# Two layers of an attention head loop: VectorE's lower parts ahead of the row maxima, and a landing copy between exponentials

## The chip, the cores and the metric

One NeuronCore of one Trainium2 chip runs the whole model in one launch. The metric is device time in microseconds (us), the median of the runs. The engines are TensorE (PE in the rows, PEld its weight loads), VectorE (DVE), ScalarE (ACT), GpSimd (POOL) and SyncE (SP), which issues the DMAs here. Each engine takes its own instructions in order and waits on semaphores for the others.

## The reference, cut to what matters

272 tokens (256 and 16 meta tokens) go through a convolution layer with a mixture of experts, an MLA attention layer with a mixture of experts, and then through two layers of a second block. The change touches MLA's first projections and, in both layers of the second block, the loop over eight sparse-attention heads:

```python
def mla_mixer(hn, w_dq, cq_g, w_uq, w_o, k_nope, k_rope, v, cos, sin):
    cq = rmsnorm(hn @ w_dq, cq_g)
    ...
for layer in range(DEPTH):                      # second block, twice
    h = rmsnorm_2(x, pre_norm[layer])
    proj = h @ w_in[layer]
    (hq, hf, hi, hz, nq, kc, vc, ks, vs, kw, vw, ng, nz) = jnp.split(proj, offsets, axis=-1)
    o_h = hgrn2_mixer(...)
    o_h = rmsnorm_2(o_h, hgrn_out_norm[layer]).reshape(B, S, HGRN_WIDTH) * jax.nn.silu(hz)
    o_n = nsa_mixer(...)                         # per head: selected and window branch
    ...                                          #   p = softmax(q k' * scale), o += gate * p v
    o_n = o_n.reshape(B, S, NSA_WIDTH) * jax.nn.silu(nz)
    y = jnp.concatenate([o_h, o_n], axis=-1) @ w_out[layer]
    x = x + rmsnorm_2(y, post_norm[layer])
```

## The kernel before

**Weights in two parts.** A weight matrix is cut into units of 128x2048 fp32. SyncE loads a unit in two halves into one of three raw slots of `ring`. ScalarE's `upper` copies each half to fp32r (the upper part, `ring_parts<-ring 128x1024`, line 1187, semaphore `w_hi`); VectorE's `lower_units` subtracts it from the raw half (the lower part, `ring_parts<-ring,ring_parts`, line 1622, semaphore `w_ready`). TensorE then makes every product of three matmuls, `mm3` (lines 532 to 534). The next load into a slot waits until TensorE has used the unit.

**MLA's start.** TensorE multiplies units 16 and 17 (counted over the kernel) by the normed chunks, sums two squares (`norm_sum`, L528), and goes on with unit 18, the third. ScalarE's `mla` takes the root (L1184), makes the upper parts of the 16 chunks as VectorE norms them (`upper_chunk`), then the upper part of unit 18 (`upper(u + 2)`), then copies and squares the first product. VectorE makes the lower part of unit 18 after its last chunk.

**The head loop** (`layer2`, once a layer). Before it, the last two of the unit tiles outside the loop are made, TensorE sums squares for the HGRN norm with four matmuls into banks 4 to 7 (`osum`), ScalarE takes the logarithm of the four banks at once (L1495, `olog`) and then the exponential of it (L1497, `oroot`). Then, for head h = 0 to 7:

- TensorE: `beside(h, 0)`, the first half (a tile) of the projection unit `IN_HEADS[h]`, into bank 7 (h below 6; in heads 6 and 7 there is output projection instead); eight transposes of the probabilities of head h (lines 1108 to 1111, after `p_ready`, signal `pt_done`); `scores(h + 2)`; `beside(h, 1)`, the second tile, again bank 7; the product with v (twelve L528 matmuls, `pv_done`). A tile into bank 7 waits until ScalarE has copied the tile before it out of the bank (`land`, signal `pj_copied`), and for the unit's lower part.
- VectorE: `tensor_copy` of half the transposes (L2151, L2152), `probs(h + 1)` (it scales the exponentials, L2136 to L2139 and an L1642 of 128x512, signal `p_ready`), `maxima(h + 2)` (four reductions L2090 and a scaling L1645, signal `mx_ready`), `lower_next(1)` (the two lower-part instructions of the unit of head h + 1), `output(h)` (L1642 128x256, after `pv_done` and the gate `z_ready`; signal `o_n`). In heads 1, 2, 4 and 5 a gating product of the HGRN output comes first (L1642 128x512, signal `o_h`).
- ScalarE: `land` of tile 0; its half of the transposes; in heads 1, 2, 4 and 5 an upper part of 128x512; `upper` of the unit two heads on; `exps(h + 2)`: four exponentials L1481, two for each branch `br`, after `mx_ready`; `land` of tile 1 (in head 0 it stands ahead of `exps`); in heads 0, 1, 3, 4 and 5 `gate`, Silu on landed tiles (L1472, signal `z_ready`); the upper part of head h's output, after `o_n`. A switch between Exp and Silu costs an ACT_TABLE_LOAD.
- GpSimd: the lower parts of the gated outputs (L1555), each after ScalarE's upper part.

Of the kernel before, what the change touches and what calls it, by code (L numbers as in the profile page):

```python
# [20 lines left out]
P = 128  # L21
D = 1024
# [172 lines left out]
def build(nc, h_in, consts_in, vecs_in, dense, experts, out):  # L195
    with ExitStack() as ctx:
# [190 lines left out]
        def wide(v):  # L387

            return v.rearrange("p a b -> p (a b)")
# [133 lines left out]
        def _(pe):  # L523
# [370 lines left out]
            def layer2(layer):  # L894
# [166 lines left out]
                for i in range(4):  # L1061
                    m = mm(psum[:, 4 + i, :], C("ones"), b_d[:, i * 512:i * 512 + 512], 0, 1)
                m.then_inc(b2["osum"], 1)
# [37 lines left out]
                for h in range(HEADS):  # L1101
                    g, n = h // 4, HEADS * layer + h
                    e, pt = n_e[h % 2], n_pt[h % 2]
                    beside(h, 0)
                    pe.wait_ge(b2["p_ready"], n + 1)
# [63 lines left out]
        def _(act):  # L1169
# [114 lines left out]
            def mla():  # L1284
                norm_root(D, T, 5, loaded=True)
                for parts, whole in ((ml_kvs, ml_kv), (ml_qs, ml_q)):
                    for c in range(DC):
                        t.next(nrm_out)
                        upper_chunk(parts, whole, c)
                u = CONV_UNITS  # L1290
                upper(u + 2)
# [110 lines left out]
            def layer2(layer):  # L1402
# [71 lines left out]
                def exps(h):  # L1474

                    _, least, total = n_st[h % 2]
                    t.next(b2["mx_ready"])
                    for br in range(2):
                        for i, at, n in ((0, 0, P), (1, P, SEQ)):
                            c = 2 * br + i  # L1480
                            m = act.activation(n_e[h % 2][:, br, at:at + n], psum[:, 2 * (h % 2) + br, at:at + n], ACT.Exp,  # L1481
                                               scale=NSA_SCALE, bias=least[:, c:c + 1], accum_out=total[:, c:c + 1])
                    m.then_inc(b2["e_done"], 1)
# [10 lines left out]
                t.next(b2["osum"])  # L1494
                act.activation(wide(b_qe), flat[:, 2048:4096], ACT.Ln, scale=1.0 / P, bias=eps[:, :]).then_inc(b2["olog"], 1)  # L1495
                t.next(b2["olog"])
                act.activation(wide(b_qe), wide(b_qe), ACT.Exp, scale=-0.5).then_inc(b2["oroot"], 1)  # L1497
                exps(1)
                for h in range(HEADS):
# [14 lines left out]
                    if h + 2 < HEADS:  # L1514
                        exps(h + 2)
                    if 0 < h < len(IN_HEADS):
                        land(*IN_HEADS[h], layer, halves=(1,), only=7)
# [88 lines left out]
        def _(v):  # L1606
# [326 lines left out]
            def layer2(layer):  # L1933
# [209 lines left out]
                for h in range(HEADS):  # L2143
# [12 lines left out]
                    if h + 1 < HEADS:  # L2156
                        probs(h + 1)
                    if h + 2 < HEADS:
                        maxima(h + 2)
                    lower_next(1)  # L2160
# [151 lines left out]
```

## Time and profile before

| | us |
|---|---|
| median of 3 runs | 1830.06 |
| lowest, highest | 1828.79, 1831.27 |
| the profiled execution, its own time | 1831.33 |
| its span | 1829.5 |
| TensorE / VectorE / ScalarE / GpSimd busy in it | 1665.1 / 831.9 / 647.7 / 60.2 |
| TensorE's mean granted clock, share of full | 0.948 |

How to read it: the profile is of one execution; times are from the start of its span. MLA's start lies at 587 to 655 us, the head loop of the second block's first layer at 1380.5 to 1463 us and that of the second layer 318.1 us later. Busy time of a pipelined TensorE runs into the next instruction: matmuls start closer than they last. The idle time in brackets is what the engine waited before the row, and the name behind it what ended the wait.

### The profile page before, as it was taken

Reading aid. Unit: us, or ns where it says so; the run is one execution under the profiler, and the core shown is the slowest. Engines: PE = TensorE matmul, PEld = TensorE weight load, DVE = VectorE, ACT = ScalarE, POOL = GpSimd, SP = SyncE. Lnnn points to the kernel's source line nnn. Section 1 sums busy time; section 2 is a strip of 40 time slices with the busy share of each in tenths; the row PEclk is TensorE's granted clock in tenths of the full one; section 3 lists DMA queues with packets and bytes.
Section 4 is the critical chain, followed back from the end, with each engine's and each line's share of the span. In section 5 each row is a group of like instructions: output and inputs, shape, how many; then the busy total and the mean of one; then the engine's idle time right before and its main releaser. Section 6 shows DMA issues by size and latency. Waiting matters only on the chain.

```text
span 1829.5 us, 30992 instructions
## 1 busy us (share of the span) xinstructions
PE 1665.1 (91%) x12314; PEld 1198.2 (65%) x12314; DVE 831.9 (45%) x1503; ACT 647.7 (35%) x1169; POOL 60.2 (3%) x58
## 2 busy tenths in 40 slices
PE   8999888887879999988888888999999999999997
PEld 8995334342425869534343333499998989999897
DVE  5652121221214764322121212388866656886663
ACT  4432111111112643211110111266557645655763
POOL 0100000000001000000000000100001110000110
PEclk9999888888989999989888989999999999999999
DMA  7769999999999524999999999935542344554232
GB/s 283 266 258 415 421 421 421 421 421 422 421 422 418 177 89 168 416 421 421 421 421 421 421 421 422 405 124 175 170 156 93 104 151 130 170 171 153 93 116 93
DMA packets 89660, 527.53 MB, mean 288 GB/s; under 512 B 10080, under 2 KB 10592, under 8 KB 40032
## 3 DMA queue, kind: packets, MB, share of 16 engines
q1 hardware_dynamic: 89568, 526.24, 73.3%
q8 instruction: 66, 1.08, 0.2%
q14 instruction: 26, 0.21, 0.0%
HBM read 525.15 MB, written 1.05 MB: 288 GB/s over the span
## 4 chain that ended last, share of the span: by engine, by line
PE 56%; DMA 26%; DVE 8%; SPq 7%; ACT 2%; issue 1%; DVEq 0%
DMA ring<-experts 25%; PE banks L528 12%; PE banks L532 10%; PE banks L534 10%; PE banks L533 10%; SPq L458 5%; PE banks L728 5%; PE banks L709 3%; PE banks L747 3%; DVE arena L1642 2%; DMA ring<-dense 1%; DVE hT L1767 1%; SPq L465 1%; DVE ring_parts L1622 1%; PE banks L589 1%
## 5 line engine op out<-in xcount | busy, mean ns | idle before, releaser
L532 PE MATMUL banks<-arena_parts,ring_parts 128*128 128x256 f32 (+1 forms) x1444 | 417.1, 289 | 8.2 <-ACT arena L1187 3.9
L534 PE MATMUL banks<-arena_parts,ring_parts 128*128 128x256 f32 (+1 forms) x1444 | 408.7, 283 | 0.0
L533 PE MATMUL banks<-arena_parts,ring_parts 128*128 128x256 f32 (+1 forms) x1444 | 408.2, 283 | 0.0
L728 PE MATMUL banks<-ring,arena 128*32 128x512 f32 x1536 | 252.7, 756 | 119.6 <-DMA ring<-experts 119.5
L528 PE MATMUL banks<-arena 128*128 128x128 f32 (+3 forms) x2416 | 322.9, 288 | 1.9 <-ACT arena L1187 1.3
L528 PEld LDWEIGHTS banks<-arena 128*128 128x128 f32 (+1 forms) x2416 | 289.9, 190 | 47.8 <-issue 35.5
L1187 ACT ACTIVATE arena<-banks 128x256 f32<-128x256 f32 (+9 forms) x366 | 156.5, 454 | 387.7 <-PE banks L740 153.4
L1622 DVE TENSOR_TENSOR ring_parts<-ring,ring_parts 128x1024 fp32r<-128x1024 f32 x204 | 245.2, 1234 | 99.4 <-ACT ring_parts L1187 87.0
L532 PEld LDWEIGHTS banks<-arena_parts,ring_parts 128*128 128x128 f32 x1444 | 272.3, 189 | 16.5 <-issue 7.3
L1187 ACT ACTIVATE ring_parts<-ring 128x1024 fp32r<-128x1024 f32 x208 | 215.3, 1055 | 181.0 <-DMA ring<-dense 179.3
L533 PEld LDWEIGHTS banks<-arena_parts,ring_parts 128*128 128x128 f32 x1444 | 272.6, 189 | 0.3
L534 PEld LDWEIGHTS banks<-arena_parts,ring_parts 128*128 128x128 f32 x1444 | 272.2, 188 | 0.0
L728 PEld LDWEIGHTS banks<-ring,arena 128*32 128x32 f32 x1536 | 39.7, 119 | 312.0 <-DMA ring<-experts 218.4
L1811 DVE TENSOR_TENSOR arena<-arena,banks 128x256 f32<-128x256 f32 x32 | 13.5, 422 | 376.2 <-ACT arena L1264 376.2
L709 PE MATMUL banks<-arena 128*128 128x272 f32 x544 | 156.2, 412 | 9.2
L1264 ACT ACTIVATE arena<-banks 128x256 f32<-128x256 f32 x32 | 12.3, 384 | 426.8 <-PE banks L728 426.8
L1767 DVE TENSOR_TENSOR hT<-hT,banks 128x272 f32<-128x272 f32 x272 | 117.6, 438 | 42.5 <-PE banks L709 36.8
L709 PEld LDWEIGHTS banks<-arena 128*128 128x128 f32 x544 | 87.1, 188 | 68.8 <-DVE hT L1767 60.6
L747 PE MATMUL banks<-arena 128*32 128x512 f32 x768 | 91.9, 596 | 0.0
L1813 DVE COPY arena<-banks 128x256 f32<-128x256 f32 x32 | 13.6, 425 | 148.0 <-PE banks L735 148.0
L1818 DVE COPY arena<-banks 128x512 f32<-128x512 f32 x32 | 22.1, 691 | 111.7 <-PE banks L747 111.7
L1555 POOL TENSOR_TENSOR arena_parts<-arena,arena_parts 128x272 fp32r<-128x272 f32 (+2 forms) x40 | 41.2, 1034 | 717.5 <-ACT arena_parts L1187 615.7
(225 smaller groups left out, 1599.3 us busy)
## 6 DMA issues: line engine op xcount, KB each, us to landing
ring<-experts SPq DMA_DIRECT2D x192, 1024.0 KB, 26.4
arena<-experts SPq DMA_DIRECT2D x144, 1024.0 KB, 22.5
ring<-dense SPq DMA_DIRECT2D x224, 512.0 KB, 4.8
at<-experts SPq DMA_DIRECT2D x16, 1024.0 KB, 25.7
consts<-experts SPq DMA_DIRECT2D x16, 1024.0 KB, 26.3
x<-experts SPq DMA_DIRECT2D x16, 1024.0 KB, 23.9
consts<-consts_in SPq DMA_DIRECT2D x2, 1024.0 KB, 15.0
vecs<-vecs_in SPq DMA_DIRECT2D x1, 1125.5 KB, 11.6
```

Source lines behind the costliest of these rows:

```text
L458: sp.dma_start(expert_slot(u), experts[layer, (pair * 2 + (odd + 1 + QUADS)) % QUADS, u]).then_inc(m[f"landed{u}"], 16)
L528: return pe.matmul(o, lhsT, rhs, start=(k == 0), stop=(k == n - 1))
L532: pe.matmul(o, lhsT[0], rhs[0], start=(k == 0), stop=False)
L533: pe.matmul(o, lhsT[0], rhs[1], start=False, stop=False)
L534: return pe.matmul(o, lhsT[1], rhs[0], start=False, stop=(k == n - 1))
L709: pe.matmul(psum[:, banks[c % len(banks)], 0:T], mo_y[:, c * P:c * P + P], mo_sw[:, 0:T], start=True, stop=True).then_inc(s["cmb_done"], 1)
L728: m = pe.matmul(psum[32 * e:32 * e + 32, 3, :], mo_xs[:, k, 32 * e:32 * e + 32], w[:, e, :], start=(k == 0), stop=(k == 7), tile_position= ...
L747: m = pe.matmul(psum[32 * e:32 * e + 32, 4 + half_, :], mo_ht[:, k, 32 * e:32 * e + 32], w[:, e, :], start=(k == 0), stop=(k == 1), tile_p ...
L1187: return act.activation(o, i, ACT.Copy)
L1555: return gp.tensor_tensor(lo, whole, hi, ALU.subtract)
L1622: v.tensor_tensor(ring_parts[:, slot, at], ring[:, slot, at], ring_parts[:, PAIRS_OF_SLOTS + slot, at], ALU.subtract).then_inc(w_ready, 1)
L1767: v.tensor_tensor(hT[:, c, :], hT[:, c, :], psum[:, banks[c % len(banks)], 0:T], ALU.add).then_inc(s["add_done"], 1)
```

## The change

The diff has five edits.

1. VectorE, head loop: `lower_next(1)` now stands ahead of `maxima(h + 2)` in every head.
2. ScalarE, head loop: for heads 1 to 5 the `land` of tile 1 stands between the exponentials of the two branches instead of after the fourth.
3. Before the loop: the four square-sum matmuls come in the order 2, 3, 0, 1 with a signal after each pair, ScalarE takes the logarithm in two halves of 1024 columns, banks 6 and 7 first, each with a signal.
4. TensorE waits for the first of these signals ahead of head 0's tile, and for the second ahead of head 0's transposes.
5. ScalarE, MLA: `upper(u + 2)` stands ahead of the 16 chunks' upper parts.

```diff
-                for i in range(4):
+                for i in (2, 3, 0, 1):
                     m = mm(psum[:, 4 + i, :], C("ones"), b_d[:, i * 512:i * 512 + 512], 0, 1)
-                m.then_inc(b2["osum"], 1)
+                    if i % 2:
+                        m.then_inc(b2["osum"], 1)
...
                     beside(h, 0)
+                    if h == 0:
+                        t.next(b2["olog"])
                     pe.wait_ge(b2["p_ready"], n + 1)
...
                 norm_root(D, T, 5, loaded=True)
+                u = CONV_UNITS
+                upper(u + 2)
                 for parts, whole in ((ml_kvs, ml_kv), (ml_qs, ml_q)):
                     for c in range(DC):
                         t.next(nrm_out)
                         upper_chunk(parts, whole, c)
-                u = CONV_UNITS
-                upper(u + 2)
...
-                def exps(h):
+                def exps(h, between=None):
...
                     for br in range(2):
+                        if br and between is not None:
+                            land(*IN_HEADS[between], layer, halves=(1,), only=7)
...
-                t.next(b2["osum"])
-                act.activation(wide(b_qe), flat[:, 2048:4096], ACT.Ln, scale=1.0 / P, bias=eps[:, :]).then_inc(b2["olog"], 1)
-                t.next(b2["olog"])
+                for part in (1, 0):
+                    t.next(b2["osum"])
+                    cut = slice(part * D, part * D + D)
+                    act.activation(wide(b_qe)[:, cut], flat[:, 2048:4096][:, cut], ACT.Ln, scale=1.0 / P, bias=eps[:, :])\
+                       .then_inc(b2["olog"], 1)
+                t.next(b2["olog"], 2)
...
                     if h + 2 < HEADS:
-                        exps(h + 2)
-                    if 0 < h < len(IN_HEADS):
-                        land(*IN_HEADS[h], layer, halves=(1,), only=7)
+                        exps(h + 2, between=h if 0 < h < len(IN_HEADS) else None)
...
                         probs(h + 1)
+                    lower_next(1)
                     if h + 2 < HEADS:
                         maxima(h + 2)
-                    lower_next(1)
                     output(h)
```

In the orders below a row is one instruction (x: so many in a row), with the semaphores that it waits for. VectorE in head 1 of the second block, before:

```order
L2136 RECIPROCAL arena<-arena 128x4 [waits b2_e_done]
L1642 TENSOR_TENSOR arena<-arena,vecs 128x4 [waits dve_chain]
L2139 TENSOR_TENSOR arena<-arena 128x2x128 [waits dve_chain]
L1642 TENSOR_TENSOR arena<-arena 128x2x256
L2090 TENSOR_REDUCE arena<-banks 128x1 [waits b2_sc_done,b2_p_ready]
L2090 TENSOR_REDUCE arena<-banks 128x1 x3
L1645 TENSOR_SCALAR arena<-arena 128x4 [waits dve_chain]
L1622 TENSOR_TENSOR ring_parts<-ring,ring_parts 128x1024 [waits w_hi,b2_mx_ready]
L1622 TENSOR_TENSOR ring_parts<-ring,ring_parts 128x1024 [waits w_hi]
L1642 TENSOR_TENSOR arena<-arena,banks 128x256 [waits b2_z_ready,b2_pv_done]
```

and now:

```order
L2142 RECIPROCAL arena<-arena 128x4 [waits b2_e_done]
L1648 TENSOR_TENSOR arena<-arena,vecs 128x4 [waits dve_chain]
L2145 TENSOR_TENSOR arena<-arena 128x2x128 [waits dve_chain]
L1648 TENSOR_TENSOR arena<-arena 128x2x256
L1628 TENSOR_TENSOR ring_parts<-ring,ring_parts 128x1024 [waits w_hi,b2_p_ready]
L1628 TENSOR_TENSOR ring_parts<-ring,ring_parts 128x1024 [waits w_hi]
L2096 TENSOR_REDUCE arena<-banks 128x1 [waits b2_sc_done]
L2096 TENSOR_REDUCE arena<-banks 128x1 x3
L1651 TENSOR_SCALAR arena<-arena 128x4 [waits dve_chain]
L1648 TENSOR_TENSOR arena<-arena,banks 128x256 [waits b2_z_ready,b2_pv_done,b2_mx_ready]
```

The two lower parts, which stood between `mx_ready` and the output product, stand between `probs` and the four reductions. ScalarE in head 1, from the table load for Exp to the upper part of the head's output (L1472 now L1475, L1481 now L1486, L1187 now L1190), before:

```order
L1481 ACT_TABLE_LOAD
L1481 ACTIVATE arena<-banks,arena 128x128 [waits b2_mx_ready]
L1481 ACTIVATE arena<-banks,arena 128x256
L1481 ACTIVATE arena<-banks,arena 128x128
L1481 ACTIVATE arena<-banks,arena 128x256
L1187 ACTIVATE arena<-banks 128x256 [waits b2_pj_done]
L1472 ACT_TABLE_LOAD
L1472 ACTIVATE arena<-arena 128x512 [waits b2_pj_copied] x2
L1187 ACTIVATE arena_parts<-arena 128x256 [waits b2_o_n]
```

and now:

```order
L1486 ACT_TABLE_LOAD
L1486 ACTIVATE arena<-banks,arena 128x128 [waits b2_mx_ready]
L1486 ACTIVATE arena<-banks,arena 128x256
L1190 ACTIVATE arena<-banks 128x256 [waits b2_pj_done]
L1486 ACTIVATE arena<-banks,arena 128x128
L1486 ACTIVATE arena<-banks,arena 128x256
L1475 ACT_TABLE_LOAD
L1475 ACTIVATE arena<-arena 128x512 [waits b2_pj_copied] x2
L1190 ACTIVATE arena_parts<-arena 128x256 [waits b2_o_n]
```

The copy out of bank 7, which waits for `b2_pj_done`, went from behind the fourth exponential to behind the second. ScalarE at MLA's start, before:

```order
L1184 ACTIVATE root<-banks,scalars 128x272 [waits nrm_sum]
L1187 ACTIVATE arena_parts<-arena 128x272 [waits nrm_out] x16
L1187 ACTIVATE ring_parts<-ring 128x1024 [waits landed0a]
L1187 ACTIVATE ring_parts<-ring 128x1024 [waits landed0b]
L1187 ACTIVATE arena<-banks 128x272 [waits mla_a_done]
L1174 ACTIVATE arena<-banks 128x272
L1187 ACTIVATE arena<-banks 128x272
```

and now:

```order
L1187 ACTIVATE root<-banks,scalars 128x272 [waits nrm_sum]
L1190 ACTIVATE ring_parts<-ring 128x1024 [waits landed0a]
L1190 ACTIVATE ring_parts<-ring 128x1024 [waits landed0b]
L1190 ACTIVATE arena_parts<-arena 128x272 [waits nrm_out] x16
L1190 ACTIVATE arena<-banks 128x272 [waits mla_a_done]
L1177 ACTIVATE arena<-banks 128x272
L1190 ACTIVATE arena<-banks 128x272
```

The two upper-part instructions of unit 18 went past sixteen chunks' upper parts. TensorE's, GpSimd's and SyncE's instructions keep their order; TensorE's waits for `olog` alone are new.

## Rows read from the trace of the kernel before

**Rows 1.** Windows; stretch: us, PE, PEld, DVE, ACT, POOL busy, clock, DMA share, GB/s.

```profile
300.00:350.00 50.00, 40.88 (x267) 19.14 (x267) 7.11 (x16) 5.53 (x9) 0.00 (x0) 0.83 1.01 422
...
1380.50:1447.00 66.50, 64.75 (x497) 60.43 (x498) 49.02 (x101) 53.86 (x120) 10.49 (x9) 1.00 0.28 91
```

**Rows 2.** Timeline of TensorE: start, us, engine, line, what, count [idle before].

```profile
1380.54 0.39 PE L532 MATMUL banks<-arena_parts,ring_parts 128*128 128x256 f32 x1 [0.36 <-ACT arena L1495]
...
1391.79 0.38 PE L532 MATMUL banks<-arena_parts,ring_parts 128*128 128x256 f32 x1 [0.77 <-DVE ring_parts L1622]
...
1413.46 0.36 PE L532 MATMUL banks<-arena_parts,ring_parts 128*128 128x256 f32 x1 [0.32 <-ACT arena L1187]
...
1421.83 2.10 PE L528 MATMUL banks<-arena 128*128 128x256 f32 x12
...
1423.87 0.39 PE L532 MATMUL banks<-arena_parts,ring_parts 128*128 128x256 f32 x1
```

**Rows 3.** Timeline of VectorE, head 2 of the first layer.

```profile
1408.11 1.78 DVE L1642 TENSOR_TENSOR arena<-arena 128x512 f32<-128x512 f32 x1
...
1409.93 1.15 DVE L2090 TENSOR_REDUCE arena<-banks 128x1 f32<-128x128 f32 x4
...
1411.32 2.36 DVE L1622 TENSOR_TENSOR ring_parts<-ring,ring_parts 128x1024 fp32r<-128x1024 f32 x2
...
1413.60 0.41 DVE L1642 TENSOR_TENSOR arena<-arena,banks 128x256 f32<-128x256 f32 x1
```

**Rows 4.** Timeline of ScalarE, heads 2 and 3.

```profile
1411.32 0.37 ACT L1481 ACTIVATE arena<-banks,arena 128x128 f32<-128x128 f32 x1 [0.33 <-DVE arena L1645]
...
1412.13 0.36 ACT L1481 ACTIVATE arena<-banks,arena 128x128 f32<-128x128 f32 x1
...
1412.92 0.39 ACT L1187 ACTIVATE arena<-banks 128x256 f32<-128x256 f32 x1
...
1422.64 0.39 ACT L1187 ACTIVATE arena<-banks 128x256 f32<-128x256 f32 x1
```

**Rows 5.** Timeline of GpSimd, head 2.

```profile
1407.87 1.48 POOL L1555 TENSOR_TENSOR arena_parts<-arena,arena_parts 128x512 fp32r<-128x512 f32 x1 [1.52 <-ACT arena_parts L1187]
```

**Rows 6.** Timeline of ScalarE, VectorE and TensorE, heads 0 and 1.

```profile
1390.51 0.37 ACT L1481 ACTIVATE arena<-banks,arena 128x128 f32<-128x128 f32 x1 [1.02 <-DVE arena L1645]
...
1395.06 0.37 ACT L1187 ACTIVATE arena<-banks 128x256 f32<-128x256 f32 x1
...
1394.29 0.42 DVE L1642 TENSOR_TENSOR arena<-arena,banks 128x256 f32<-128x256 f32 x1 [1.41 <-ACT arena L1472]
...
1395.89 0.56 DVE L2151 COPY arena<-banks 128x384 f32<-128x384 f32 x1 [0.39 <-PE banks L1111]
...
1397.29 0.37 PE L532 MATMUL banks<-arena_parts,ring_parts 128*128 128x256 f32 x1
```

**Rows 7.** Timeline of TensorE and ScalarE ahead of the loop.

```profile
1374.89 3.60 PE L528 MATMUL banks<-hT,consts 128*128 128x512 f32 x8
...
1378.52 1.97 ACT L1495 ACTIVATE arena<-banks,scalars 128x2048 f32<-128x2048 f32 x1 [1.75 <-PE banks L528]
```

**Rows 8.** MLA's start: ScalarE, VectorE, TensorE, SyncE's issues; landing of the ring's DMAs, 560:612.

```profile
594.08 0.84 ACT L1187 ACTIVATE arena_parts<-arena 128x272 fp32r<-128x272 f32 x2 [2.56 <-DVE arena L1633]
...
606.13 1.99 ACT L1187 ACTIVATE ring_parts<-ring 128x1024 fp32r<-128x1024 f32 x2
...
607.27 2.36 DVE L1622 TENSOR_TENSOR ring_parts<-ring,ring_parts 128x1024 fp32r<-128x1024 f32 x2 [0.57 <-ACT ring_parts L1187]
...
608.74 1.30 PE L528 MATMUL banks<-arena,consts 128*128 128x272 f32 x4 [1.33 <-ACT arena L1174]
...
609.69 0.48 PE L532 MATMUL banks<-arena_parts,ring_parts 128*128 128x272 f32 x1
...
570.87 2.71 SPq L413 DMA_DIRECT2D ring<-dense  x6
...
DMA to landing us min/median/max: 3.9/8.2/11.9
```

## The prediction

> **What bounds the kernel now.** The page's busy times (the table above) name TensorE, with every other engine below half. The windows then separate the stages. In the expert loops the DMA share is 1.01 and TensorE's granted clock 0.83; in the head loop the DMA share is 0.28, the clock 1.00, and TensorE is busy 64.75 of 66.50 us while ScalarE has 53.86 and VectorE 49.02 [rows 1]. So the head loop is bound by TensorE, with two engines behind it that have little room in each head. Its timeline shows what it still waits for. With no wait a tile starts 0.06 us before the modelled end of the matmuls ahead of it: 1421.83 + 2.10 = 1423.93, and the tile of head 4 starts at 1423.87. A wait therefore costs the idle time shown plus 0.06: 0.42 us at head 0 (the logarithm), 0.83 at head 1 (the lower part), and 0.38 at head 3 (the copy out of bank 7), with the same at heads 2 and 5 to 0.01, which are not shown [rows 2]. That is 2.4 us a layer, and all that the edits in the loop can win, 4.8 in both layers. The sum is made on the first layer and doubled, since the second showed the same five waits to 0.05 us, 318.1 us later.
>
> **VectorE's lower part ahead of the maxima.** In head 2 VectorE's last scaling ends at 1409.89, the reductions start at 1409.93, and `mx_ready` comes just before 1411.32, when both ScalarE's exponentials and VectorE's lower parts start; the exponentials had waited 0.33 for it. The output product follows the lower parts at 1413.60, so these occupy 1413.60 - 1411.32 = 2.28 us [rows 3, 4]. Put ahead, they delay `mx_ready` by 2.28. ScalarE was waiting already, so its exponentials go from 1411.32 to 1413.60. Nothing hides this: the cover would be ScalarE's own arrival, and it arrives early by 0.33, in heads 0 and 3 by about 1.0 [rows 4, 6].
>
> **The copy between the exponentials.** Two exponentials with their accumulator reads take 1412.13 - 1411.32 = 0.81; the copy came 1412.92 - 1411.32 = 1.60 after the first [rows 4]. It now comes 0.79 earlier in that sequence. The tile that it copies is complete by then (TensorE is in the products with v). Net for the copy: 2.28 - 0.79 = 1.49 us later. Where TensorE already waited for it, TensorE pays the 1.49 in full: the stalls of 0.38 at heads 3 and 5 become 1.87. At head 4 the copy ended at 1422.64 + 0.39 = 1423.03 and TensorE starts 0.15 after such an end (1412.92 + 0.39 = 1413.31, and 1413.46), so the room was 1423.87 - 1423.18 = 0.69 and the loss is 1.49 - 0.69 = 0.80 [rows 2, 4]. Heads 3 to 5 together: 1.49 + 0.80 + 1.49 = 3.8.
>
> **Heads 0 and 1.** The split logarithm lets head 0's tile go: the first pair of square sums, half of the 3.60 us from 1374.89, is ready near 1376.8, a logarithm of 1024 columns is about half of 1.97, so bank 7 is free near 1377.9, ahead of the tile's 1380.1 [rows 7]. Gain 0.42, of which the transposes, which wait for probabilities that did not move, leave 0.40. With the lower part early the 0.83 of head 1 goes too: TensorE reaches that tile 1.22 sooner. But exponentials of head 2 wait for later maxima: VectorE is 0.40 sooner and then 2.28 later, so they start at 1390.51 + 1.88 = 1392.4. Behind them in ScalarE's queue stand the table load and the gate's Silu, for which VectorE's output of head 0 waited already (1.41 us until 1394.29); it moves by 1.88, and so does everything behind it on both engines [rows 6]. ScalarE's copy out of bank 7 for head 1's second tile goes from 1395.06 to about 1396.7, ends at 1397.1, and TensorE may start at 1397.25. It would have come at 1397.29 - 1.22 = 1396.07, so it stands 1.2 us, and the 1.22 won is spent: head 1's second tile starts where it did. VectorE's copies in head 1 start near 1397.2 rather than 1395.89 (+1.3), because output and gating product were late [rows 6]. So the maxima in that head are 1.3 + 2.28 = 3.6 late, the copy 3.6 - 0.79 = 2.8, and head 2's tile 2.8 later than now. GpSimd's 1.48 us instruction overlaps VectorE's 128x512 scaling and this lasts 1.78 [rows 3, 5]; in head 1 the later start lets it catch the 128x256 scaling as well, for which I add 0.2. Net at head 2: 3.0, a stall of about 3.4 instead of 0.37.
>
> **In order, or not.** The output product at 1413.60 starts only after the lower parts although TensorE had ended head 2 by 1413.46 - 0.32 = 1413.14 [rows 2, 3]: VectorE takes the queue as written. The Trainium skill ("TensorE: Matmul & The Clock Gate", the section on the array of 16 x 32x32) says that ACT's and DVE's queues are strict FIFO; the trace agrees. If VectorE could pass the lower parts, the sum would be that of the first rival.
>
> **MLA's third unit.** ScalarE idles 2.56 us before its first chunk at 594.08, and the upper part that fills it takes 1.99 [rows 8]. Its data must have landed: the ring's six transfers for the first three units were issued from 570.87 on, within 2.71 us, and those of this stretch land within 11.9 us of their issue, so by 585.5, ahead of the idle time's start at 591.5. ScalarE's squares then start at 606.13 instead of 1.9 later, and the square sums no longer wait 1.33. But unit 18's matmuls began at 609.69, right behind VectorE's lower part, 607.27 + 2.36 = 609.63. VectorE can start 0.57 + 0.08 = 0.65 sooner, directly behind its last chunk (0.08 is what one instruction runs into the next: 1411.32 + 2.36 - 1413.60, [rows 3]), and that is the gain: 0.65, not 1.33 [rows 8]. Later waits in MLA are for TensorE's own progress or for transfers that this triggers, so they shift along; the expert transfers too start on TensorE's signals.
>
> **The sum.** A layer: heads 0 and 1 give 0.0, head 2 costs 3.0, heads 3 to 5 cost 3.8, heads 6 and 7 have no tile in bank 7, and their output projection needs none of this: +6.8. Two layers +13.6, MLA -0.65: **+13.0 us**. The profiled execution's own time of 1831.33 becomes 1844.3; it is at the top of the three runs, so I take the median: 1830.06 + 13.0 = **1843.0 us**.
>
> **Bounds of what the trace does not show.** Three things are not in a row. Whether the late gate of head 0 reaches head 1 fully: if not, head 1 keeps its 1.22, head 2 costs 1.49, and a layer costs 4.0 instead of 6.8. Whether GpSimd's instructions fall on the lower parts in their new place: the Trainium skill ("SBUF — State Buffer", Who interferes with whom) says that a VectorE instruction with two SBUF inputs contends with a GpSimd instruction that reads SBUF, and by it a lower part could be held as the scaling was, to which GpSimd's 1.48 us is the bound. From the rows themselves, GpSimd ends at 1409.35 and the scaling at 1409.89, so I put nothing; the upper bound is one such meeting more in a layer, which stays within the range. And the clock, below.
>
> **Rivals.**
> - *Faster: the maxima are not missed.* Were ScalarE late enough that a `mx_ready` 2.28 later cost nothing, all five stalls would go: 1830.06 - 4.8 - 0.65 = 1824.6. It decides at an idle time of ScalarE before the exponentials of zero and maxima ready 2.3 ahead; the rows show the opposite, 0.33 and 1.02 of waiting [rows 4, 6]. For it speaks only that the gain in head 1 may be kept.
> - *Only the direct delay.* The gate chain of heads 0 and 1 is absorbed: two layers at 4.0, less 0.65, is +7.4: 1837.4. Against it: VectorE waited 1.41 for that gate already.
> - *The clock falls.* TensorE stands for 3.4 us at head 2, four times its longest wait inside the loop now. In the expert loop, with 40.88 of 50 us busy, the granted clock is 0.83, a mix of 2.4 and 1.2 GHz; in the head loop it is 1.00 [rows 1]. If 7 us of matmuls, two thirds of a head (a length that I assume), ran at the lower level, half of it, some 3.5 us, would come on top in a layer: 1846.5 for one layer, 1850.0 for both. Against it: on both sides of the stalls TensorE is dense.
> - *It comes out even.* The waits overlap so that the loop costs about what MLA and the removed stalls give, within 3.6 us of 1830.06. No row supports it.
>
> **How the numbers follow.** The forecast 0.68 (its own range 1840 to 1846), the direct delay alone 0.12, the clock 0.10, faster 0.05, even 0.05. The range 1837 to 1848 holds the forecast, the direct delay and one fall of the clock. 0.2%, about 3.7 us, is what a measurement can tell from no change: faster 0.05, same 0.05, slower 0.90.
>
> **What would show it.** VectorE's reductions start behind the lower parts, 2.3 us after the scaling's end, and ScalarE waits about 2.6 us before the exponentials of heads 1, 2 and 4. TensorE waits for the copy (ACT L1190) ahead of the tiles: about 3.4 us at head 2, 1.9 at heads 3 and 5, 0.8 at head 4, and 1.2 ahead of head 1's second tile; the waits for L1495 and for VectorE's lower part are gone. The loop from head 0's tile to head 6 is 6.8 to 7.2 us longer in each layer. In MLA the 1.33 before the square sums is gone and a wait of about 0.6 for the lower part stands behind them. Wrong would be: ScalarE not waiting for `mx_ready`, or exponentials late but the tile's copy early.

## The result, and the profile after

The changed kernel's median is 1852.13 us (1851.65 to 1852.61, four runs), against 1829.6 for the kernel before (four runs): a ratio of 1.0118, with a 95% interval of 1.0106 to 1.0130. The forecast was 1843.0 with a range up to 1848. The sign was right. The loss was 22.5 us (by the medians) instead of 13.0, and the time lies 4.1 us above the range. The profiled execution took 1851.78 us, 20.45 more than the profiled one of before, and has a span of 1850.0.

TensorE's waits in the first layer's head loop, by the view of waits (1378 to 1470 us; engine and line, releaser: total, times, longest):

```profile
PE banks L532 <- ACT arena L1190: 8.6, 5, 3.2
```

Before it was 0.9 in three waits for ScalarE's copy, 0.8 for a lower part and 0.4 for the logarithm. The last two are gone and the copy out of bank 7 is the only thing waited for. The rows that answer to [rows 2], TensorE's timeline (head 1's second tile, head 2, head 3; then head 2 in the second layer):

```profile
1396.17 0.39 PE L532 MATMUL banks<-arena_parts,ring_parts 128*128 128x256 f32 x1 [1.13 <-ACT arena L1190]
...
1404.44 0.55 PE L532 MATMUL banks<-arena_parts,ring_parts 128*128 128x256 f32 x1 [3.25 <-ACT arena L1190]
...
1419.30 0.36 PE L532 MATMUL banks<-arena_parts,ring_parts 128*128 128x256 f32 x1 [1.78 <-ACT arena L1190]
...
1734.63 0.55 PE L532 MATMUL banks<-arena_parts,ring_parts 128*128 128x256 f32 x1 [3.24 <-ACT arena L1190]
```

Heads 4 and 5 wait 0.66 and 1.78, and the second layer shows the same five to 0.03. What makes them is in the rows that answer to [rows 3, 5, 6] and [rows 4]. VectorE in heads 0 and 1, with the GpSimd instruction that meets it, then ScalarE:

```profile
1387.52 2.36 DVE L1628 TENSOR_TENSOR ring_parts<-ring,ring_parts 128x1024 fp32r<-128x1024 f32 x2
1389.80 1.14 DVE L2096 TENSOR_REDUCE arena<-banks 128x1 f32<-128x128 f32 x4
...
1394.97 0.42 DVE L1648 TENSOR_TENSOR arena<-arena,banks 128x256 f32<-128x256 f32 x1 [3.83 <-ACT arena L1475]
...
1397.25 1.56 DVE L2145 TENSOR_TENSOR arena<-arena 128x256 f32<-128x256 f32 x1
...
1399.45 2.36 DVE L1628 TENSOR_TENSOR ring_parts<-ring,ring_parts 128x1024 fp32r<-128x1024 f32 x2
1401.73 1.14 DVE L2096 TENSOR_REDUCE arena<-banks 128x1 f32<-128x128 f32 x4
```

```profile
1397.23 1.30 POOL L1561 TENSOR_TENSOR arena_parts<-arena,arena_parts 128x512 fp32r<-128x512 f32 x1 [0.48 <-ACT arena_parts L1190]
```

```profile
1391.18 0.37 ACT L1486 ACTIVATE arena<-banks,arena 128x128 f32<-128x128 f32 x1 [3.25 <-DVE arena L1651]
...
1403.11 0.37 ACT L1486 ACTIVATE arena<-banks,arena 128x128 f32<-128x128 f32 x1 [2.76 <-DVE arena L1651]
...
1403.92 0.38 ACT L1190 ACTIVATE arena<-banks 128x256 f32<-128x256 f32 x1
```

The lower parts stand ahead of the four reductions, ScalarE waits 3.25 and 2.76 for `mx_ready` where it waited 1.02 and 0.32, and VectorE's output product of head 0 waits 3.83 for the gate instead of 1.41. The copy comes 0.81 behind the first exponential (1403.92 - 1403.11), and TensorE's 3.25 end behind it. GpSimd's instruction lies on VectorE's 128x256 scaling, which takes 1.56; where the two don't meet (head 0), it takes 0.42.

So far this is the forecast. What it left out is in the windows (columns as in [rows 1]; the first row is the same stretch of the kernel before, the others are the kernel after):

```profile
1403.10:1409.90 6.80, 6.80 (x58) 6.46 (x57) 3.90 (x8) 5.79 (x11) 2.48 (x2) 1.00 0.27 104
```

```profile
1403.10:1409.90 6.80, 5.46 (x25) 5.49 (x26) 1.11 (x2) 4.73 (x13) 1.01 (x1) 0.52 0.11 43
1420.20:1423.60 3.40, 3.40 (x19) 3.40 (x18) 0.00 (x0) 0.07 (x1) 0.73 (x1) 0.53 0.01 5
1444.00:1447.40 3.40, 3.10 (x15) 3.13 (x16) 0.40 (x1) 3.18 (x8) 0.12 (x1) 0.55 0.28 112
1734.50:1737.90 3.40, 3.27 (x15) 3.30 (x16) 0.04 (x1) 3.37 (x8) 0.00 (x0) 0.50 0.02 5
1748.00:1751.40 3.40, 3.04 (x14) 3.07 (x15) 0.00 (x0) 1.33 (x6) 0.73 (x1) 0.52 0.29 118
```

At heads 2, 3 and 5 of the first layer and at heads 2 and 3 of the second, the granted clock is 0.50 to 0.55 in these windows, its level of 1.2 GHz. It falls somewhere between 1.1 us ahead of the end of the wait (head 2, first layer) and 1.2 us behind it (head 3, first layer). In the kernel before it is 1.00 all through both loops. Outside what is left of the wait TensorE stays full (3.40 of 3.40 us at head 3) and gets through fewer matmuls. In the first stretch it is 25 instead of 58, with 1.34 us of waiting in it. The timeline shows the same, two matmuls at each level:

```profile
1398.86 0.28 PE L533 MATMUL banks<-arena_parts,ring_parts 128*128 128x256 f32 x1
1398.97 0.28 PE L534 MATMUL banks<-arena_parts,ring_parts 128*128 128x256 f32 x1
...
1405.01 0.41 PE L534 MATMUL banks<-arena_parts,ring_parts 128*128 128x256 f32 x1
1405.22 0.41 PE L532 MATMUL banks<-arena_parts,ring_parts 128*128 128x256 f32 x1
```

They start 0.11 to 0.12 us apart at 2.4 GHz and 0.21 to 0.22 at 1.2 GHz.

The time from one head's first transpose to the next head's shows what each wait and each stretch costs (in us, heads 0 to 7, from TensorE's timelines; the row of before is its first layer, the second shows the same to 0.04):

| | 0-1 | 1-2 | 2-3 | 3-4 | 4-5 | 5-6 | 6-7 | sum |
|---|---|---|---|---|---|---|---|---|
| before, both layers | 11.28 | 10.82 | 10.82 | 10.41 | 10.80 | 7.51 | 8.67 | 70.31 |
| after, layer 1 | 10.46 | 17.39 | 13.95 | 11.28 | 13.80 | 7.52 | 8.67 | 83.07 |
| after, layer 2 | 10.44 | 16.53 | 13.70 | 11.16 | 12.32 | 7.48 | 8.67 | 80.30 |

The loops grew by 12.76 and 9.99, together 22.75. The first transpose of layer 1 came 1.61 earlier and 0.68 were won between the layers: 22.75 - 1.61 - 0.68 = 20.46, the whole difference of the two profiled executions. But the one of after had reached MLA's first matmul 1.75 us earlier (593.38 against 595.13), ahead of every edit, and in the twelve profiled executions of this document that point lies anywhere from 592.70 to 595.33. Without these 1.75 the change costs 22.2, about what the medians say (22.5). In MLA the chain is as forecast, TensorE's wait for the square sums replaced by a shorter one behind them ([rows 8]):

```profile
607.27 0.40 PE L532 MATMUL banks<-arena_parts,ring_parts 128*128 128x272 f32 x1 [0.69 <-DVE ring_parts L1628]
```

The stretch from 595.13 (MLA's first matmul) to the wait at 645.03 took 49.90 before and 593.38 to 642.30 takes 48.92 now. But here too the clock falls, in MLA's next part:

```profile
652.60:656.00 3.40, 3.40 (x13) 2.45 (x13) 0.00 (x0) 0.40 (x1) 0.00 (x0) 0.52 0.52 159
```

### The profile page after: what moved, and what is told of

Read it like the earlier page. It is cut to its first block, busy times and chain, and to the rows that moved or that the text cites. A ratio compares the mean times of both kernels' runs of the same rounds, so it can differ in the third digit from the quotient of the medians.

```text
span 1850.0 us, 30984 instructions
## 1 busy us (share of the span) xinstructions
PE 1674.5 (91%) x12314; PEld 1207.5 (65%) x12314; DVE 831.4 (45%) x1503; ACT 647.4 (35%) x1171; POOL 60.1 (3%) x58
## 4 chain that ended last, share of the span: by engine, by line
PE 55%; DMA 26%; DVE 9%; SPq 6%; issue 2%; ACT 2%; DVEq 0%
DMA ring<-experts 25%; PE banks L528 12%; PE banks L532 10%; PE banks L534 10%; PE banks L533 9%; SPq L458 5%; PE banks L728 5%; PE banks L709 3%; PE banks L747 3%; DVE ring_parts L1628 2%; DVE arena L1648 2%; DMA ring<-dense 1%; DVE hT L1773 1%; SPq L465 1%; DVE arena L2096 1%
## 5 line engine op out<-in xcount | busy, mean ns | idle before, releaser
L532 PEld LDWEIGHTS banks<-arena_parts,ring_parts 128*128 128x128 f32 x1444 | 276.2, 191 | 30.4 <-issue 20.7
L1190 ACT ACTIVATE arena<-banks 128x256 f32<-128x256 f32 (+9 forms) x366 | 156.2, 453 | 391.1 <-PE banks L740 153.3
L1190 ACT ACTIVATE ring_parts<-ring 128x1024 fp32r<-128x1024 f32 x208 | 215.2, 1055 | 179.1 <-DMA ring<-dense 177.7
L533 PEld LDWEIGHTS banks<-arena_parts,ring_parts 128*128 128x128 f32 x1444 | 276.6, 192 | 0.3
L534 PEld LDWEIGHTS banks<-arena_parts,ring_parts 128*128 128x128 f32 x1444 | 276.2, 191 | 0.0
## 6 DMA issues: line engine op xcount, KB each, us to landing
arena<-experts SPq DMA_DIRECT2D x144, 1024.0 KB, 22.5
```

The lines of the kernel that those rows point to most:

```text
L532: pe.matmul(o, lhsT[0], rhs[0], start=(k == 0), stop=False)
L533: pe.matmul(o, lhsT[0], rhs[1], start=False, stop=False)
L534: return pe.matmul(o, lhsT[1], rhs[0], start=False, stop=(k == n - 1))
L1190: return act.activation(o, i, ACT.Copy)
```

## The experiments

The theory after the result: the waits are those of the forecast, +13, and the rest is the lower clock behind them. Its rivals: that the waits cost more than was summed up (the gate chain of heads 0 and 1, GpSimd), that the other edits cost something, and that MLA's edit brings the clock down there.

**Edit 1 undone.**

```diff
-                    lower_next(1)
                     if h + 2 < HEADS:
                         maxima(h + 2)
+                    lower_next(1)
```

> The changed kernel with its first edit undone: VectorE takes the maxima ahead of the lower parts again, the other four edits stay. Theory S (late maxima cause TensorE's stalls, and the stalls pull the clock down): the logarithm's wait (0.42 us) and the three waits for the copy out of bank 7 (0.38 each) are gone, head 1's wait for the lower part (0.83) stays; 1.6 us a layer and 0.65 in MLA, so 1829.6 - 3.9 = 1825.7 us, no low clock in the head loops. Rival T (the copy between the exponentials or the split logarithm does harm of its own): 1829.6 us or more, with new waits for ScalarE ahead of tiles.

Measured: 1826.61 us (11 runs), ratio 0.998 (0.9971 to 0.9989). The only wait left in the loop is head 1's:

```profile
1389.18 0.39 PE L532 MATMUL banks<-arena_parts,ring_parts 128*128 128x256 f32 x1 [0.77 <-DVE ring_parts L1628]
```

The clock is 1.00 in both loops. So edit 1 alone carries the loss, and the other four together are a small gain. In the kernel before, the copy behind the fourth exponential ended waits of TensorE at heads 2, 3 and 5; with the copy between the exponentials these three waits are gone.

**Edit 1 alone, on the kernel before.**

```diff
+                    lower_next(1)
                     if h + 2 < HEADS:
                         maxima(h + 2)
-                    lower_next(1)
```

> The kernel before with the first edit alone: lower parts ahead of the maxima, the copy out of bank 7 still after the fourth exponential. Theory S: the copy is 2.28 us late instead of 1.49, so TensorE waits about 4.2 us at head 2, 2.7 at heads 3 and 5, 1.6 at head 4, 1.2 in head 1 and 0.42 at head 0; 10.4 us a layer, 1850.4 us with a full clock, and 1858 to 1864 with falls of the clock at least as long as in the changed kernel. Rival T (it is the other edits that hurt): 1826 to 1835 us.

Measured: 1863.93 us (4 runs), ratio 1.0192 (1.0176 to 1.0207). The view of waits, 1378 to 1470, and a window behind the longest:

```profile
PE banks L532 <- ACT arena L1187: 11.8, 5, 4.0
```

```profile
1404.00:1411.40 7.40, 4.83 (x24) 4.86 (x25) 1.48 (x4) 4.73 (x13) 1.00 (x1) 0.54 0.15 60
```

The clock is down here too. The copy behind the fourth exponential stands 0.79 later, and heads 2, 3, 4 and 5 wait 4.04, 2.57, 1.47 and 2.61, about 0.8 more each than in the kernel after. The early copy softens edit 1, it is not a part of the harm. The clock falls at seven of the eight long waits: behind 4.04, 2.57, 1.47 and 2.61 in the first layer, and behind 4.04, 1.50 and 2.57 in the second, but not behind head 3's 2.61 there.

**The waits of 2, 3 and 5 filled with unread matmuls.** What tells waits and clock apart.

```diff
+                    keep_clock(4, {2: 3, 3: 2, 5: 2}.get(h, 0))
                     beside(h, 0)
```

> The changed kernel, with matmuls that nobody reads put on TensorE where it stands: three of 128x512 fp32 ahead of head 2's tile, two ahead of head 3's and head 5's, into bank 4, whose transposes have been copied out by then (0.86 us each). They compute nothing new. Theory S: TensorE stays busy, the waits that remain are 0.7 us or less, the granted clock stays 1.00 in both head loops, and the 8.3 us that the low clock cost there come back: 1852.1 - 8.3 = 1843.8 us; the heads last what the waits alone give, 6.8 us a layer over the kernel before. Rival L (the lower parts in their new place slow TensorE's or VectorE's work in another way, the clock only goes along with it): 1852 us or more.

Measured: 1843.76 us (4 runs), ratio 1.0071 (1.0056 to 1.0087). TensorE at head 2 (one of these matmuls is two rows of the trace, so three are x6), and the window there:

```profile
1400.62 2.84 PE L528 MATMUL banks<-consts 128*128 128x512 f32 x6
1403.90 0.36 PE L532 MATMUL banks<-arena_parts,ring_parts 128*128 128x256 f32 x1 [0.44 <-ACT arena L1191]
```

```profile
1403.90:1410.70 6.80, 6.80 (x55) 6.46 (x56) 3.33 (x7) 6.45 (x14) 2.47 (x2) 1.00 0.01 2
```

The tile still can't start before the copy, so the critical chain is untouched, but the clock is 1.00 in both loops. From first transpose to first transpose a layer takes 77.46 (10.46, 15.08, 12.27, 11.18, 12.28, 7.52, 8.67), 7.15 more than before. This is the forecast's sum, and 1843.76 its time. It is 8.4 us below the kernel after; by the sums of the periods the clock cost 83.07 - 77.46 = 5.6 in one layer and 80.30 - 77.46 = 2.8 in the other. The rival that the waits themselves cost more than was summed up falls.

**Only one of the two groups filled.** Does head 2's long wait bring the clock down for the later heads too, or does each wait act by itself? First heads 3 and 5 are left open, then head 2:

```diff
+                    keep_clock(4, {2: 3}.get(h, 0))
...
+                    keep_clock(4, {3: 2, 5: 2}.get(h, 0))
```

> The changed kernel with the filling matmuls of e3 ahead of head 2's tile alone (three); the waits of 1.8 us at heads 3 and 5 stay open. Theory P (one long wait of 3.25 us is what pulls the clock down, the later falls follow from it): the clock stays 1.00 in both loops, as e3, 1843.8 us. Theory Q (each wait of 1.8 us can do it by itself): some low clock of 3.4 us after heads 3 and 5 in each layer, 1.7 us for each, 1846 to 1850 us.

> The changed kernel with the filling ahead of the tiles of heads 3 and 5 alone (two each); the wait of 3.25 us at head 2 stays open. Theory P: nearly all of the low clock stays, 1850 to 1852 us. Theory Q: the low clock after head 2 stays (3.4 to 6.8 us a layer), that after heads 3 and 5 goes, 1847 to 1850 us.

Measured: 1848.42 (1843.44 to 1849.6) and 1849.15 us (1845.67 to 1850.85), 4 runs each, ratios 1.0091 (1.0073 to 1.0109) and 1.0103 (1.0087 to 1.0120). With head 2 filled, the layers differ: in the first, waits of 1.78 at heads 3 and 5 leave the clock at 1.00; in the second both are followed by the lower level. With head 2 filled, head 3 of the first layer and the window behind it, then the windows at heads 3 and 5 of the second:

```profile
1417.51 0.36 PE L532 MATMUL banks<-arena_parts,ring_parts 128*128 128x256 f32 x1 [1.78 <-ACT arena L1191]
```

```profile
1417.50:1420.90 3.40, 3.39 (x29) 3.39 (x30) 0.00 (x0) 1.24 (x6) 0.74 (x1) 1.00 0.18 75
```

```profile
1743.50:1746.90 3.40, 3.40 (x19) 3.40 (x19) 0.00 (x0) 0.00 (x0) 0.73 (x1) 0.53 0.01 5
1767.50:1770.90 3.40, 3.40 (x16) 3.40 (x17) 0.69 (x1) 2.86 (x7) 0.43 (x1) 0.51 0.24 92
```

With heads 3 and 5 filled, the window behind head 2 of the second layer and then the stretch over head 3:

```profile
1731.10:1734.50 3.40, 3.40 (x19) 3.40 (x18) 0.69 (x1) 2.37 (x5) 1.00 (x1) 0.51 0.02 5
1740.00:1760.00 20.00, 19.33 (x138) 16.93 (x137) 10.43 (x27) 11.37 (x33) 1.73 (x2) 1.00 0.33 106
```

Each wait acts by itself: those of heads 3 and 5 need no fall at head 2, and head 2's fall does not outlast its own stretch. The theory that head 2 alone was the cause missed 4.6 us on the first of the two.

**Head 0 with its maxima first.** The forecast derived 1.2 at head 1's second tile and the size of head 2's wait from head 0's late gate.

```diff
-                    lower_next(1)
+                    if h:
+                        lower_next(1)
                     if h + 2 < HEADS:
                         maxima(h + 2)
+                    if not h:
+                        lower_next(1)
```

> The changed kernel with maxima first in head 0 alone; heads 1 to 5 keep the lower parts first. It tests the chain through head 0's gate. Theory S: the exponentials, the gate and the output product of head 0 are as early as before, no wait ahead of head 1's second tile; TensorE waits 0.83 at head 1 (the lower part), 1.9 at heads 2, 3 and 5 and 0.8 at head 4: 4.9 us a layer instead of 6.8, 1838.7 us with a full clock, and up to 1846 with the low clock after the waits of 1.8 us. Rival (the 3.25 us wait at head 2 has its cause in head 1, not in head 0): head 2 still waits over 3 us, 1852 us.

Measured: 1844.22 us (1840.70 to 1847.28, 4 runs), ratio 1.0083 (1.0068 to 1.0098). VectorE waits 1.40 for the gate of head 0, as in the kernel before, instead of 3.83, and TensorE at head 2 waits as at head 3:

```profile
1391.06 0.42 DVE L1648 TENSOR_TENSOR arena<-arena,banks 128x256 f32<-128x256 f32 x1 [1.40 <-ACT arena L1475]
```

```profile
1400.86 0.36 PE L532 MATMUL banks<-arena_parts,ring_parts 128*128 128x256 f32 x1 [1.80 <-ACT arena L1190]
1413.11 0.43 PE L532 MATMUL banks<-arena_parts,ring_parts 128*128 128x256 f32 x1 [1.77 <-ACT arena L1190]
```

The wait ahead of head 1's second tile is gone, and head 2's is 1.80 instead of 3.25. The gate chain is confirmed. In this execution the clock falls behind the waits that end at 1413.11 and 1737.20, and not behind the other four of the same length (1400.86, 1438.06, 1724.92, 1762.18). The window behind 1413.11:

```profile
1413.30:1416.70 3.40, 3.40 (x17) 3.40 (x17) 0.00 (x0) 0.77 (x4) 0.73 (x1) 0.51 0.13 54
```

The other three runs, which took longer, were not profiled.

**Head 0's norm scaling behind the lower part.** With edit 1 undone, one wait was left. In head 0 VectorE's instruction of 128x2048, 2.35 us long, stands ahead of the lower part, and nothing on TensorE needs it so soon.

```diff
-                    if h == 0:
-                        t.next(b2["oroot"])
-                        stt(wide(b_ke), wide(b_ke), V(f"on{layer}"), wide(b_qe), ALU.mult, ALU.mult)
...
-                    lower_next(1)
                     if h + 2 < HEADS:
                         maxima(h + 2)
+                    lower_next(1)
+                    if h == 0:
+                        t.next(b2["oroot"])
+                        stt(wide(b_ke), wide(b_ke), V(f"on{layer}"), wide(b_qe), ALU.mult, ALU.mult)
```

> Maxima first as in e1, and in head 0 the scaling of the HGRN output by its norm (2.33 us on VectorE) goes from ahead of the probabilities to behind the lower part. Nobody needs it before the gating product of head 1. Theory S: head 1's wait for the lower part (0.83 us) goes too, no wait of the head loop is left: 2.45 us a layer and 0.65 in MLA, 1829.6 - 5.6 = 1824.0 us. Rival T: the later norm makes the gating product and the copies of head 1 late, a new wait of 1 us or more stands ahead of head 2's tile, and it is no better than e1, 1825.7 us.

Measured: 1824.67 us (7 runs), ratio 0.9971 (0.9959 to 0.9982). VectorE in head 0, and the windows of both layers:

```profile
1387.67 2.36 DVE L1628 TENSOR_TENSOR ring_parts<-ring,ring_parts 128x1024 fp32r<-128x1024 f32 x2
1389.95 2.35 DVE L1654 SCALAR_TENSOR_TENSOR arena<-arena,vecs 128x2048 f32<-128x2048 f32 x1
```

```profile
1380.50:1447.00 66.50, 66.36 (x513) 62.06 (x513) 51.00 (x104) 55.29 (x125) 11.18 (x10) 1.00 0.29 96
1698.60:1765.10 66.50, 66.50 (x514) 62.35 (x515) 50.74 (x97) 53.36 (x121) 11.19 (x10) 1.00 0.28 96
```

No wait is left in either loop: TensorE is busy 66.36 and 66.50 of 66.50. It has the lowest median of the study, 0.3% below the kernel before; its interval overlaps that of edit 1 undone (0.9971 to 0.9989), so the last wait's share, 1.94 us by the medians for 0.77 + 0.73 of waiting and 0.06 on each, is not proved by the times alone.

**MLA's edit by itself, and taken out again.** The clock's fall near 653 stood in the kernel after and not before, so the edit was suspected.

```diff
                 norm_root(D, T, 5, loaded=True)
+                u = CONV_UNITS
+                upper(u + 2)
                 for parts, whole in ((ml_kvs, ml_kv), (ml_qs, ml_q)):
...
-                u = CONV_UNITS
-                upper(u + 2)
```

> The kernel before with the MLA edit alone (the third unit's upper part ahead of the chunks). In the changed kernel and in e1, e3 and e4, which all have this edit, TensorE's clock was low for some 3.5 us from 652 us on, in the kernel before and in e2, without it, it was not. Theory M (the edit shifts MLA's waits by 1.0 us against whatever grants the clock, and the clock falls with the same waits): the wait before the square sums goes, MLA's head 0 comes 1.0 us sooner, the clock is low from about 652 to 655.5, which costs 1.6 us, and the time is 1829.6 + 0.6 = 1830.2 us, no gain. Rival N (the fall comes from the head loops' edits or from chance): clock 1.00 there, 1828.6 us.

> e4 with the MLA edit undone. Theory M: the clock stays 1.00 in MLA, the gain of the two head loops stands alone: 1829.6 - 4.9 = 1824.7 us or a little less than e4 (1824.7 measured there). Rival N: 0.65 to 1.0 us slower than e4, 1825.5 us.

Measured: alone 1831.01 us (10 runs), ratio 1.0003 (0.9993 to 1.0012); the kernel of the last section without it 1825.73 us (11 runs), ratio 0.9976 (0.9967 to 0.9985). The windows, with the edit alone and with all but it:

```profile
653.50:656.90 3.40, 3.40 (x15) 3.25 (x16) 0.11 (x1) 0.96 (x3) 0.00 (x0) 0.52 0.09 17
```

```profile
652.50:655.90 3.40, 3.40 (x15) 3.16 (x14) 0.00 (x0) 0.50 (x3) 0.00 (x0) 0.50 0.26 71
```

The clock falls without the edit as well, so the suspicion falls. In all of them two waits of TensorE stand 8 us apart, near 642 to 645 (1.29 to 1.47) and near 650 to 653 (1.19 to 1.40). Of the profiled executions without a fill there, the eight with a fall had the second wait end between 650.0 and 652.4, but so had one without a fall (651.44, head 2 filled); the two others without one had it end at 652.75 (edit 1 alone) and 653.16 (the kernel before). The fall does not hang on the edit; what it hangs on is open. Its price is the same in all: from the second wait to TensorE's wait near 733 it takes 82.15 to 82.34 us in the eight executions with a fall and 80.67 to 80.72 in the others, so 1.6 us.

**MLA's second wait filled.**

```diff
+                    if h == 0:
+                        keep_clock(5, 1)
```

> e4 with one matmul of 128x512 fp32 that nobody reads (0.86 us) into bank 5 ahead of MLA's first transposes, where TensorE waits 1.3 us for VectorE. Theory M: the clock stays 1.00 in MLA, 1824.7 - 1.6 = 1823.1 us. Rival N: the same as e4.

Measured: 1825.67 us (10 runs), ratio 0.9975 (0.9966 to 0.9985), against 1824.67 without the fill. The clock stayed at 1.00 and the wait shrank to 0.54, but no time was won in the medians. The expectation of a gain was wrong. In the profiled executions the stretch behind the wait did get shorter (80.67 against 82.15 without the fill), but the one with the fill had reached MLA 1.56 us later (595.30 against 593.74), ahead of any difference between the two kernels. Why the medians show nothing is open: some of the unprofiled runs without the fill may have had no fall either, and a gain of 1.6 is small against the spread of each kernel's runs (3.4 and 5.6 us).

## Why the prediction was right or wrong

**Maxima, exponentials, copy: right.** ScalarE waits 2.76 where 2.6 was said, the copy stands 0.81 behind the first exponential (0.79 to 0.81), and heads 3, 4 and 5 wait 1.78, 0.66 and 1.78. With 0.06 each that is 1.84, 0.72 and 1.84 against 1.87, 0.80 and 1.87. Edit 1 undone showed that the copy alone removes the waits of heads 2, 3 and 5.

**Heads 0 and 1: the chain is right, its two sizes came out partly by luck.** The waits for the logarithm and the lower part went, and 1.13 stands ahead of head 1's second tile (1.2). Head 2 waits 3.25 (3.4). The run with head 0's maxima first showed that both come from head 0's gate. GpSimd caught the 128x256 scaling (1.56 instead of 0.42), but then let the 128x512 one go (0.68, where it took 1.78 in head 1 before). From the first of these two to what follows them it takes 1399.45 - 1397.25 = 2.20, before it took 2.16: nothing, where the forecast had added 0.2. What made up for it is a start that the forecast put too early: from head 0's first exponential to VectorE's copies in head 1 it took 5.38 before (1395.89 - 1390.51) and takes 5.01 (1396.19 - 1391.18), so these copies are 1.88 - 0.37 = 1.5 late and not 1.3, and the 3.0 at head 2 comes out. In the same way ScalarE's copy for head 1's second tile belongs at 1395.06 + 1.88 = 1396.94, not at 1396.7, by which the wait would have been 1.4. And a tile behind L1030 starts 0.19 and not 0.06 ahead of that row's end (1397.26 + 0.22 - 1397.29), so the waits at head 0 and ahead of head 1's second tile cost 0.13 more each than the forecast's rule says. The Trainium skill ("SBUF — State Buffer", Who interferes with whom) says that a VectorE instruction with two SBUF inputs contends with a GpSimd one that reads SBUF; these rows agree. The lower parts stayed at 2.36, which was the forecast.

**The sum of waits: right.** 6.8 to 7.2 a layer was said, 7.15 was measured with the clock kept up in the loops, and the time of that kernel is 1843.76 against 1843.0. That the time comes so close is partly chance, since its clock still falls in MLA.

**MLA: right as a chain, too small to be seen.** The first part took 0.98 less (49.90 - 48.92, 0.65 forecast); over all profiled executions it is 48.79 to 49.12 in the nine with the edit and 49.59 to 49.90 in the three without. But the lower clock in the next part gave more back in that execution: from 653.16 to 733.88 it took 80.72 before, from 650.41 to 732.70 it takes 82.29, +1.57. In the median of ten runs the edit alone is +0.03% with an interval of 0.1% on either side.

**The clock: wrong, and this is nearly the whole miss.** The failed step is the clock. The sum put it at nothing, and the rival "The clock falls" got a chance of 0.10, on the ground that "on both sides of the stalls TensorE is dense". It was no ground. TensorE was dense before and after every one of these waits and the clock fell all the same, five times in the two loops of the profiled execution. The rival counted too few stretches, only head 2's, and took 3.5 us for it. Head 2's fall cost 2.31 in the first layer (17.39 - 15.08), less because its first 1.1 us lay in the wait, and heads 3 and 5 cost 1.68 and 1.52 there (13.95 - 12.27 and 13.80 - 12.28). In the second layer heads 2 and 3 cost 1.45 and 1.43. Together that is 5.5 and 2.9, 8.4 us. The fall in MLA is 1.57 more, by which MLA lost 0.6 in the profiled execution where 0.65 of gain was forecast. With 13.0 + 8.4 the time would have been 1851.5.

The kernel before had no wait above 0.8 in the head loop, so no row of that loop priced a wait of 2 or 3 us. But its trace has rows that speak of it elsewhere, of which the prediction used only the mean clock of 0.83. In an expert loop TensorE waits 0.99 and then 1.42 us for transfers:

```profile
507.81 1.07 PE L728 MATMUL banks<-ring,arena 128*32 128x512 f32 x8 [0.99 <-DMA ring<-experts]
510.30 1.93 PE L728 MATMUL banks<-ring,arena 128*32 128x512 f32 x8 [1.42 <-DMA ring<-experts]
```

```profile
510.30:513.70 3.40, 2.85 (x16) 0.40 (x16) 0.00 (x0) 0.00 (x0) 0.00 (x0) 0.50 1.02 424
```

Behind the second wait the clock is 0.50 and the same eight matmuls take 1.93 instead of 1.07. Waits come every 2.5 us there, so these rows don't say what a single one does in a dense loop, and in MLA of the same execution waits of 1.35 and 1.32 left the clock at 1.00. They did say that waits of 1.4 us, and not only of 3.4, can be followed by a fall. The term needed a bound of its own, half of a stretch for each new wait, and not a single rival with one place.

## What to carry to other kernels

On an in-order engine a pair of instructions that one engine needs soon must not be put ahead of a short result that starts another engine's chain: 2.3 us of lower parts ahead of 1.4 us of maxima cost 17 us in waits (1843.76 against 1826.61 with the maxima first), of which the other edits hid 3 to 4, and 8.4 more by the clock, while the lower part was late only in one head, and moving the one long instruction ahead of it out of its way removed that wait. If an edit makes new waits on a TensorE that ran at its full clock, and they are as long as those here that were followed by a fall (1.5 us and more), let the range hold the price of a stretch at half clock for each of them. Filling such a wait with unread matmuls separates the two terms in one run, and here it won back 8.4 of the 22.5 us.

## What the runs showed of the hardware

A single wait inside a dense loop is enough to bring TensorE's clock from 2.4 to 1.2 GHz. Of 14 waits of 1.77 to 1.80 us in the loops of three profiled kernels (after, head 0's maxima first, head 2 filled) seven were followed by the lower level, and seven were not. All four waits of 3.24 or 3.25 (after, heads 3 and 5 filled) and both of 4.04 (edit 1 alone) were. In edit 1 alone three of its four waits of 2.57 or 2.61 and both of 1.47 and 1.50 were as well. So the length alone does not decide between 1.47 and 2.61 us. No wait of 1.12 to 1.16 (ten in five kernels) was followed by a fall. Such a stretch lasted 3.4 us, or 6.8 in three cases (head 2 of the first layer in the kernel after, heads 2 and 5 of it in edit 1 alone), with 0.50 to 0.55 in the windows shown and TensorE full outside the rest of the wait itself. It cost 1.4 to 2.3 us of time in the kernel after. The same wait at the same place went either way from one layer to the next (1.78 at head 5: 1444.30 with a fall, 1773.22 without), so such a wait has no fixed price.

The Trainium skill ("TensorE: Matmul & The Clock Gate", What's actually happening) says that the gate lets through either half or all of the clock pulses, and that how many matmuls run at the lower level at a kernel's start differs from run to run. The rows agree with the two levels: slices of 0.1 us around these waits show 0.50 or 1.00, but for those in which the level changes. The second no run here shows, since each kernel was profiled once. Within one run the moment does differ: with heads 3 and 5 filled, the level fell 0.4 us ahead of the end of head 2's wait in the first layer (1403.86) and 1.3 us behind it in the second (1729.84).
